# Two transformer blocks on one core: projections of the delta rule spaced with empty steps, SiLU as one ScalarE operation, and five moves of weight products

## The chip, the cores and the metric

The kernel runs on one core of a Trainium2 chip. The metric is the device time of one execution in microseconds (us), the median over runs. In the text PE is the matrix engine (TensorE), PEld its weight load, ACT the scalar engine, DVE the vector engine, POOL the GpSimd engine and SP the queue that issues transfers.

## What is computed

Two transformer blocks in series on a sequence of 512 tokens with 1024 features, all in float32. The first block has stick-breaking attention, forgetting attention and a memory attention, merged by gates, and an MLP. The change touches only the second block, which is, cut to what matters:

```
h  = rmsnorm(x)
qa, ka, va, za, alpha, beta, qb, kb, vb, ga, gb = split(h @ w_in)
qa, ka, va = silu(causal_conv4(qa, ka, va))            # 8 heads of 128, silu(x) = x * sigmoid(x)
oa = gated_deltanet(qa, ka, va, alpha, beta)           # chunks of 64: S = a S + k^T (v - k S)
oa = rmsnorm(oa) * silu(za)
ob = band_attention(qb, kb, vb, bias)                  # 16 heads of 64
x += (sigmoid(ga) * (oa @ w_a_out) + sigmoid(gb) * (ob @ w_b_out)) @ w_o
x += memory_cross_attention(rmsnorm(x), rmsnorm(mem))  # 4 heads of 256, 256 memory tokens
x += (silu(gate) * up) @ w_down
```

## The kernel before

Every weight product is one `Gemm`: a tile of 128 output features by 512 tokens, summed over eight blocks of 128 input features. Float32 accuracy comes from three passes for each block, with weights and activations split in a high and a low part: lines 1034 (high by high), 1036 (weights high, activations low) and 1040 (weights low, activations high). Weights come in units of eight blocks. SP loads a unit into `stage`, ACT makes the high part (line 1477, `whi`), and DVE or POOL subtracts to make the low part (`wlo`); in the delta rule it is POOL (line 2331). The split of the next unit stands in the queues of ACT and POOL at the first block of a product.

The order of the work is written out by hand. `Schedule` yields steps, which are lists of operations with a name; a step can be an empty list. Every engine walks the same flat list and takes its part of each operation, so the queue of every engine has the order of the list. `mix` takes one step from each of its parts in turn. `par` makes lists of its parts and spreads each evenly over their common length, so that it is the number of steps in each list, empty ones too, that decides which operation stands beside which. A product has four `mm` steps (two blocks, six matmuls each) and one `ev` step, the eviction from PSUM on DVE.

For the delta rule `block2` (line 807 on) runs nine rounds. Round h holds in one `par`: `gdn_scan(h-1)` with 24 steps, `gdn_prep(h)` with 13 and `gdn_proj(h+1)` with 45. Round 0 has no scan, round 7 has instead of a projection a few gate products, round 8 has the last scan and five gate products.

- `gdn_scan`: for each of eight chunks `gc_w` (two matmuls of the state with wt and with qd on PE, then on DVE `cuu`, line 1855) and `gc_s` (two matmuls with ckd and cuu on PE, then on DVE the new state `cs`, line 2213 or 1858). Each needs the one before, through DVE. Below W2 is `gc_w` of chunk 2, S2 its `gc_s`. Then comes a norm and the product with silu(z) on POOL.
- `gdn_prep`: `gp_kk`, `gp_xy`, five times `gp_P` and `gp_Y` (16 or 32 small matmuls on PE, then multiplications and subtractions on tiles `ya` on DVE), and `gp_uw`, 32 matmuls. Below P1 and Y1 are the first pair. With P1 go the scores of q and k, and on DVE `ceg`, `cqd` and `cpt`.
- `gdn_proj`: `products` yields the products of k, q, v and z in this order; `chain`, mixed with it, yields empty steps until a product is there, then the convolution `conv` on DVE in two steps (lines 2130 and 1858: part 0 has one `tensor_scalar` and one `scalar_tensor_tensor`, part 1 two of the latter), `silus` and the norms `hn_sq`, `hn_mm`, `hn_out` of k and q. `silus` gives a `sig` step (ACT, line 1722, into the buffers `ce`) and a `silu` step for each item (POOL, line 2331, times the sigmoid). `later(h-1)` is the one for v and z of the head before.

The scan's `gc_w` and `gc_s` share PSUM bank 7 with the norms of k and q.

Around the delta rule: `gdn_scalars` turns the alpha and beta columns, after one first product, into decays; `gdn_in` with its small matmuls opens it. `gated("a2")` with `opened` multiplies the delta output with `w_a_out`; `opened` starts two products up to their sixth block, since the last two blocks need the last head. In the band attention eight pairs of heads run each beside the three products of the next pair; pairs 3 to 7 have also one or two gate products (`raw_gate`). In `xattn` all 16 key and value products of the memory run first; then four heads of cross attention, the first two of them beside the query products of heads 2 and 3.

Of the kernel before, what the change touches and what calls it, by code (L numbers as in the profile page):

```python
# [12 lines left out]
ACT = mybir.ActivationFunctionType  # L13
# [358 lines left out]
class Schedule:  # L372
# [15 lines left out]

    def raw_gate(self, name, col, out, ph):

        return self.gemm(name, col, range(8), ("H", ph), "h", None, [("dve_ev", (name, col, 0))], extra=[Use(f"raw{col}", [])], out=out)

    def gate(self, name, col, out, place, ph):
        return self.gemm(name, col, range(8), ("H", ph), "gate", place, [("dve_ev", (name, col, 0))], out=out)
# [194 lines left out]
    def gated(self, tag, ph, gates, branches, bufs, pre, late=False):  # L589
        n, mg = 0, {"b1": "mg1", "b2": "mg2"}.get(tag)  # L590
        if tag == "a2":
            yield from self.opened(tag, branches, bufs, pre)
        for m in range(2 if tag == "a2" else 0, 8):
            A = bufs[2 + m % 2]
            uA = Use(f"{tag}acc{m % 2}", [("gt_copy", m)] if tag == "a2" else [("sp_hi", (mg, m)), ("sp_lo", (mg, m))])
            for j, ((gname, gcol), (bname, src, nk)) in enumerate(zip(gates, branches)):
                gkey, bkey = (gname, gcol + 128 * m, 0), (bname, 128 * m, 0)
                s, t_ = pre.get((m, j), (bufs[n % 2], f"{tag}s{n % 2}"))[0], bufs[4 + n % 2]
                if late and (m, j) in pre:
                    yield [st("late_gate", (gkey, s))]  # L600
                if (m, j) not in pre:
                    yield from self.gate(gname, gcol + 128 * m, s, Use(f"{tag}s{n % 2}", [("dve_ev", bkey)]), ph)
                ut = Use(f"{tag}t{n % 2}", [("gt_add", (tag, m, j))])
                yield from self.gemm(bname, 128 * m, range(nk), src, "branch", uA if j == 0 else ut, [("dve_ev", bkey)],
                                     s=s, A=A, t=t_, j=j, tag=tag, m=m, s_key=gkey)
                n += 1
            ref = ("gt_add", (tag, m, len(gates) - 1)) if len(gates) > 1 else ("dve_ev", bkey)
            yield [st("merge", (tag, m, A, ref))]

    def opened(self, tag, branches, bufs, pre):  # L610

        (bname, src, nk), made = branches[0], []
        for m in range(2):
            A, bkey = bufs[2 + m], (bname, 128 * m, 0)
            g = self.gemm(bname, 128 * m, range(nk), src, "branch", Use(f"{tag}acc{m}", [("gt_copy", m)]), [("dve_ev", bkey)],
                          s=pre[m, 0][0], A=A, t=None, j=0, tag=tag, m=m, s_key=("w_in_2", 7184 + 128 * m, 0))
            made.append((g, [st("merge", (tag, m, A, ("dve_ev", bkey)))]))
        for g, _ in made:
            yield from islice(g, nk // 2 - 1)
        for g, merge in made:  # L620
            yield from g
            yield merge
# [64 lines left out]

    def gdn_scalars(self):
        u = Use("b5", [("gs_be", 0)])
        yield [st("gs_in", u, u)]  # L690
        yield from repeat([], 5)
        u = Use("b7", [("gs_er", 0)])
        yield [st("gs_cols", u, u)]
        ub, ub2 = Use("b7", [("gs_row", 0)]), Use("b6", [("gs_row", 1)])
        rows = [Use(f"gbc{h}", self.gbc_freed(h)) for h in range(2)]
        yield [st("gs_rows", (ub, ub2), ub, ub2)]
        yield from repeat([], 8)
        yield [st("gs_store", None)] + [st("gdn_rows", (h, rows[h]), rows[h]) for h in range(2)]
# [4 lines left out]
    def gdn_proj(self, h):  # L703

        k, s = self.k, h % 2
        done = set()
        ce = [0]

        def silus(*items):
            us = []  # L710
            for e, (n, g, buf, ref) in enumerate(items):
                us.append(Use(f"ce{e}", [("silu", (n, g))]))
            yield [st("sig", (items, us), *us), st("tables", None)]
            for e, (n, g, buf, ref) in enumerate(items):
                yield [st("silu", (n, g, buf, e))]

        def later(g):
            return silus(("v", g, k.g3[g % 2]["v"], ("conv", ("v", g))), ("z", g, k.gz[g % 3], ("dve_ev", ("w_in_2", 3072 + 128 * g, 0))))
        if h == 8:
            yield [x for s_ in later(7) for x in s_]  # L720
            for _ in range(5):
                yield []
            return

        def products():
            for n in "kqv":
                j, x = "qkv".index(n), CX[n]
                yield from self.proj("w_in_2", 128 * (8 * j + h), k.cx[x][:, 3:3 + T], Use(f"cx{x}", [("conv", (n, h))]), "mix2")
                done.add(n)
            yield from self.proj("w_in_2", 3072 + 128 * h, k.gz[h % 3][:], Use(f"gz{h % 3}", [("gs_oz", h)]), "mix2")  # L730

        freed = {"q": [("pe_qk", h), ("gp_qd", h)], "k": [("pe_ktr", h)], "v": [("pe_vtr", h)]}

        def conv(n):
            while n not in done:
                yield []
            u = Use(f"g{n}{s}", freed[n])
            yield [st("conv", (n, h, 0, u), u)]
            yield [st("conv", (n, h, 1, None))]

        def unit(n, g):
            b = k.g3[s][n][:]
            return self.norm(("l2" + n, h), b, None, b, ("silu", (n, h)), k.cf("ones"), 1.0, g)

        def chain():
            yield from conv("k")
            if h:
                yield from later(h - 1)
            yield from conv("q")
            yield from silus(*((n, h, k.g3[s][n], ("conv", (n, h))) for n in "kq"))  # L750
            yield from unit("k", 1.0)
            yield from conv("v")
            yield from unit("q", 128 ** -0.5)
        yield from mix(products(), chain())
# [52 lines left out]
    def block2(self):  # L807
# [32 lines left out]

        early = {}

        def gates(*ms):
            for m in ms:
                early[m, 0] = k.bgate[m][:], None
            return [(self.raw_gate("w_in_2", 8208 + 128 * m, k.bgate[m][:], "mix2"), None) for m in ms]
        beside = [[], [], [], gates(0), gates(1), gates(2), gates(3), gates(4, 5)]

        def band_loads(p):
            for h in (2 * p, 2 * p + 1):  # L850
# [37 lines left out]
    def xattn(self):  # L888
        k = self.k
        yield [st("tables", None)]  # L890

        def proj(i):
            for j in range(2):
                s = 2 * (i % 3) + j
                yield from self.proj("w_mq_2", 256 * i + 128 * j, k.xq[s][:], Use(f"xq{s}", [("pe_xo", (i, 1)), ("pe_xo", (i, 3))]), "x2")
        yield from par(seq(proj(0), proj(1)), self.mem_norm(2, "norm_mem_2"))
        yield from self.mem_kv(2, "w_mkv_2", k.raw2, 8, k.mk2, k.mv2, None, range(16))
        self.xo = [[Use(f"b{6 + j}", [("o_hi", ("o3", 2 * i + j)), ("o_lo", ("o3", 2 * i + j))]) for j in range(2)] for i in range(4)]
        for i in range(4):
            yield from par(self.cross(i, 0), self.cross(i, 1), *([proj(i + 2)] if i < 2 else []))  # L900
            yield [st("xa_out", i)]
        yield from self.residual("w_mo_2", "o3", range(8), "ffn", "norm_ffn_2", ("w_mq_2", 896, 0))
        yield [st("fence", "ff2")]
# [551 lines left out]
def scalar_program(k, act):  # L1455
# [261 lines left out]

    def sigmoids(items, uses):
        for e, (n, g, buf, ref) in enumerate(items):
            free(uses[e])  # L1720
            wait(ref)
            act.activation(k.ce[e][:], buf[:], ACT.Sigmoid).then_inc(*up("sig", (n, g)))

    def prep_eg(h, u):
        free(u["eg"])
# [590 lines left out]
def pool_program(k, pool):  # L2316
# [64 lines left out]
        pool.wait_ge(*at("dc_sub", (h, mask)))  # L2381
        tt(k.gD, k.gD, k.cb(mask), ALU.add).then_inc(*up("dc_mask", (h, mask)))

    def silu(n, g, buf, e):
        pool.wait_ge(*at("sig", (n, g)))
        tt(buf[:], buf[:], k.ce[e][:], ALU.mult).then_inc(*up("silu", (n, g)))

    def scan_gate(h):
        wait(("silu", ("z", h)))
# [4 lines left out]
    for kind, a in k.order:  # L2394
# [7 lines left out]
        elif kind == "ev":  # L2402
            evict(a)
        elif kind == "merge":
            merge(*a)
        elif kind == "decay":
            decay(*a)
        elif kind == "silu":
            silu(*a)
        elif kind == "gs_oz":  # L2410
            scan_gate(a)
        elif kind == "band_load":
            h, _ = a
            pool.wait_ge(*at("ld_band%d" % (h % 4), h))
            pool.memset(k.band[h % 4][0:64, 0:64], NEG).then_inc(*up("band", h))
        elif kind == "fence":
            for e in ("pe", "act", "dve"):
                if k.tails.get((a, e)):
                    name, n = k.tails[a, e]
                    pool.wait_ge(k.sem(name), n)  # L2420
            k.tails[a, "pool"] = hand.tail
# [159 lines left out]
```

## Time and profile before

| what | value |
|---|---|
| median of 3 runs | 2320.1 us (2319.35 to 2322.78) |
| the profiled execution | 2320.81 us |
| its span, first to last instruction | 2319.0 us |
| granted clock of PE, mean | 0.996 |
| busy: PE, DVE, ACT, POOL | 97%, 49%, 39%, 19% |
| the chain that ended last | PE 87%, DVE 6%, ACT 3%, issue 2%, DMA 1% |
| the first block, to the fence `gdn` | to about 936 us |
| delta rule | about 936 to 1385 us |
| output product of the delta rule | about 1385 to 1430 us |
| band attention | about 1432 to 1675 us |
| products of the memory's keys and values | about 1780 to 1845 us |
| cross attention | about 1845 to 1902 us |

A row of the timeline gives the start in us from the beginning of the span, the duration in us, the engine, the line, the operation, what it writes and reads, how many instructions are merged in it, and in brackets how long the engine was idle before it and on which instruction that wait ended. A busy PE counts the tail of a matmul too, so that an idle time is given some 0.1 us too short. Which of PE's two clock levels was granted is the column PEclk: 1.00 is 2.4 GHz, 0.50 is 1.2 GHz.

### The profile page before, as it was taken

How to read it: one execution, taken by the hardware profiler on the slowest of the kernel's cores; microseconds unless marked ns; L12 is line 12 of the kernel's file. 1: busy time of each engine (PE TensorE's matmuls, PEld its weight loads, DVE VectorE, ACT ScalarE, POOL GpSimd, SP SyncE). 2: the span in 40 equal slices, each digit the busy share in tenths (PEclk: the TensorE clock that was granted, in tenths of full speed). 3: DMA queues.
4: the chain of work that ended last, by engine and by line, in shares of the span. 5: the costliest groups of instructions: out<-in, count | busy, mean ns of one | idle time of the engine just before them, and what ended most of it. 6: DMA issues, size and time to landing. Idle time of an engine off the chain costs nothing.

```text
span 2319.0 us, 32779 instructions
## 1 busy us (share of the span) xinstructions
PE 2254.3 (97%) x13098; PEld 1798.2 (78%) x13098; DVE 1141.5 (49%) x1949; ACT 892.9 (39%) x1427; POOL 443.7 (19%) x300
## 2 busy tenths in 40 slices
PE   8999999999999999999999999999999999999998
PEld 6776777888888888777777777777788988888886
DVE  4433454444544445575666512555546445435444
ACT  5544564233322223434443442444434434222223
POOL 2332221001201102444353332000011001101001
PEclk9999999999999999999999999999999999999999
DMA  4223212323333233221121123222232513233322
GB/s 166 73 64 101 64 46 82 100 92 99 93 98 101 92 99 92 95 71 47 47 70 51 38 66 128 81 82 83 63 100 92 155 37 100 91 100 100 98 93 82
DMA packets 58358, 198.95 MB, mean 86 GB/s; under 512 B 6736, under 2 KB 6864, under 8 KB 57952
## 3 DMA queue, kind: packets, MB, share of 16 engines
q1 hardware_dynamic: 58208, 196.86, 27.0%
q8 instruction: 105, 1.72, 0.3%
q14 instruction: 45, 0.37, 0.1%
HBM read 194.67 MB, written 2.16 MB: 85 GB/s over the span
## 4 chain that ended last, share of the span: by engine, by line
PE 87%; DVE 6%; ACT 3%; issue 2%; DMA 1%; POOL 0%; SPq 0%; DVEq 0%; ACTq 0%; POOLq 0%
PE bank L1034 24%; PE bank L1040 24%; PE bank L1036 24%; PE bank L989 13%; PE bank L992 2%; ACT whi L1477 1%; DMA stage<-in_wall 1%; DVE ya L1855 1%; DVE gk L1858 1%; DVE wlo L1855 0%; DVE gk L2130 0%; DVE sbA L2032 0%; SPq L2430 0%; DVE gq L1858 0%; DVE gv L1858 0%
## 5 line engine op out<-in xcount | busy, mean ns | idle before, releaser
L1034 PE MATMUL bank<-hh,whi 128*128 128x512 f32 x1680 | 688.0, 410 | 1.1 <-ACT nm1r L1517 0.6
L1040 PE MATMUL bank<-hh,wlo 128*128 128x512 f32 x1680 | 658.1, 392 | 4.8 <-DVE wlo L1855 3.1
L1036 PE MATMUL bank<-hl,whi 128*128 128x512 f32 x1680 | 656.0, 390 | 0.0
L1477 ACT ACTIVATE whi<-stage 128x1024 fp32r<-128x1024 f32 x340 | 357.3, 1051 | 326.5 <-PE bank L1040 315.5
L1855 DVE TENSOR_TENSOR wlo<-stage,whi 128x1024 fp32r<-128x1024 f32 x252 | 331.5, 1316 | 295.6 <-ACT whi L1477 295.1
L1040 PEld LDWEIGHTS bank<-hh,wlo 128*128 128x128 f32 x1680 | 315.9, 188 | 75.9 <-DVE wlo L1855 5.7
L1034 PEld LDWEIGHTS bank<-hh,whi 128*128 128x128 f32 x1680 | 316.5, 188 | 73.2 <-issue 9.3
L1036 PEld LDWEIGHTS bank<-hl,whi 128*128 128x128 f32 x1680 | 316.8, 189 | 63.6 <-issue 5.3
L2331 POOL TENSOR_TENSOR wlo<-stage,whi 128x1024 fp32r<-128x1024 f32 x88 | 210.6, 2393 | 408.1 <-ACT whi L1477 408.1
L1855 DVE TENSOR_TENSOR x<-bank,x 128x512 f32<-128x512 f32 x80 | 55.3, 691 | 152.6 <-PE bank L1040 152.6
L2331 POOL TENSOR_TENSOR acc<-acc,sqb 128x512 f32<-128x512 f32 x34 | 45.2, 1329 | 288.9 <-ACT sqb L1490 288.9
L1034 PE MATMUL bank<-u1h,whi 128*128 128x512 f32 x256 | 99.6, 389 | 0.0
L1036 PE MATMUL bank<-u1l,whi 128*128 128x512 f32 x256 | 99.6, 389 | 0.0
L1040 PE MATMUL bank<-u1h,wlo 128*128 128x512 f32 x256 | 99.6, 389 | 0.0
L2331 POOL TENSOR_TENSOR u1l<-f1t,u1h 128x512 fp32r<-128x512 f32 x32 | 41.3, 1292 | 265.2 <-ACT u1h L1575 265.2
L2331 POOL TENSOR_TENSOR u2l<-f2s,u2h 128x512 fp32r<-128x512 f32 x22 | 28.4, 1293 | 299.7 <-ACT u2h L1584 299.7
L989 PEld LDWEIGHTS bank<-ya 64*64 64x64 f32 (+1 forms) x2048 | 58.9, 138 | 32.2 <-issue 16.5
L989 PE MATMUL bank<-ya 64*64 64x64 f32 (+2 forms) x2048 | 72.4, 231 | 5.9 <-DVE ya L1855 5.8
L1575 ACT ACTIVATE u1h<-f1t 128x512 fp32r<-128x512 f32 x32 | 20.2, 632 | 126.6 <-DVE f1t L1855 126.6
L1036 PE MATMUL bank<-u2l,whi 128*128 128x512 f32 x176 | 68.6, 390 | 0.0
L1034 PE MATMUL bank<-u2h,whi 128*128 128x512 f32 x176 | 68.5, 389 | 0.0
L1040 PE MATMUL bank<-u2h,wlo 128*128 128x512 f32 x176 | 68.5, 389 | 0.0
(374 smaller groups left out, 3446.4 us busy)
## 6 DMA issues: line engine op xcount, KB each, us to landing
stage<-in_wall SPq DMA_DIRECT2D x340, 512.0 KB, 3.6
band<-in_toep SPq DMA_DIRECT2D x16, 256.0 KB, 3.9
x<-in_xT SPq DMA_DIRECT2D x8, 256.0 KB, 5.2
fb<-rowsf SPq DMA_DIRECT2D x8, 256.0 KB, 3.7
gbc<-rows SPq DMA_DIRECT2D x8, 256.0 KB, 3.3
gbc<-rowsc SPq DMA_DIRECT2D x16, 128.0 KB, 3.6
out_y<-fout SPq DMA_DIRECT2D x8, 256.0 KB, 2.3
memx<-in_memT SPq DMA_DIRECT2D x1, 1024.0 KB, 10.0
```

Source lines behind the costliest of these rows:

```text
L989: return pe.matmul(out, w, r, start=start, stop=stop, skip_group_check=True)
L992: return pe.transpose(out, in_, k.cf("ident"))
L1034: pe.matmul(o, wh, hi, start=j == 0, stop=False)
L1036: pe.matmul(o, wh, lo, start=False, stop=False)
L1040: i = pe.matmul(o, wl, hi, start=False, stop=end)
L1477: act.activation(k.whi[u % NSPLIT][:], k.stage[u % NSTAGE][:], ACT.Copy).then_inc(*up("whi", u))
L1575: act.activation(k.u1[0][:, a["t"] % 16, :], a["b"][:], ACT.Copy).then_inc(*up("sp_hi", ("u1", a["t"])))
L1855: return dve.tensor_tensor(out, a, b, op)
L1858: return dve.scalar_tensor_tensor(out=out, in0=a, scalar=s, in1=b, op0=op0, op1=op1)
L2331: return pool.tensor_tensor(out, a, b, op)
```

## The change

1. `raw_gate` uses PSUM bank 7 instead of the two banks that the products take in turn, and the six gate products beside the band attention are cut in pieces: three steps beside each of the pairs 0 to 6, nine beside pair 7.
2. `opened` starts four products instead of two, in banks 2 to 5.
3. `gdn_scalars` starts three steps later.
4. `silus` is one step: ACT applies `Silu` in place, POOL does nothing.
5. In `products` two empty steps stand after each of the products of k, q and v, for all heads but the first.
6. The value products 12 to 15 of the memory run beside cross head 0, and the query products of heads 2 and 3 beside cross heads 1 and 2.

```diff
     def raw_gate(self, name, col, out, ph):
...
+                         bank="b7", out=out)
...
-        for m in range(2 if tag == "a2" else 0, 8):
+        for m in range(4 if tag == "a2" else 0, 8):
...
     def opened(self, tag, branches, bufs, pre):
-        for m in range(2):
+        for m in range(4):
+            A, bkey = bufs[2 + m % 2], (bname, 128 * m, 0)
...
+                          bank=f"b{2 + m}", s=pre[m, 0][0], ...
...
     def gdn_scalars(self):
         u = Use("b5", [("gs_be", 0)])
+        yield from repeat([], 3)
         yield [st("gs_in", u, u)]
...
         def silus(*items):
             us = []
-            for e, (n, g, buf, ref) in enumerate(items):
-                us.append(Use(f"ce{e}", [("silu", (n, g))]))
-            yield [st("sig", (items, us), *us), st("tables", None)]
-            for e, (n, g, buf, ref) in enumerate(items):
-                yield [st("silu", (n, g, buf, e))]
+            yield [st("sig", (items, us)), st("tables", None)]
...
                 done.add(n)
+                if h:
+                    yield from repeat([], 2)
...
-        def gates(*ms):
-            for m in ms:
+        def gates():
+            for m in range(6):
                 early[m, 0] = k.bgate[m][:], None
-            return [(self.raw_gate("w_in_2", 8208 + 128 * m, k.bgate[m][:], "mix2"), None) for m in ms]
-        beside = [[], [], [], gates(0), gates(1), gates(2), gates(3), gates(4, 5)]
+                yield from self.raw_gate("w_in_2", 8208 + 128 * m, k.bgate[m][:], "mix2")
+        slow = gates()
+        beside = [[(islice(slow, 3), None)] for _ in range(7)] + [[(slow, None)]]
...
-        yield from self.mem_kv(2, "w_mkv_2", k.raw2, 8, k.mk2, k.mv2, None, range(16))
+        yield from self.mem_kv(2, "w_mkv_2", k.raw2, 8, k.mk2, k.mv2, None, range(12))
+        beside = [self.mem_kv(2, "w_mkv_2", k.raw2, 8, k.mk2, k.mv2, None, range(12, 16)), proj(2), proj(3), []]
...
-            yield from par(self.cross(i, 0), self.cross(i, 1), *([proj(i + 2)] if i < 2 else []))
+            yield from par(self.cross(i, 0), self.cross(i, 1), beside[i])
...
     def sigmoids(items, uses):
-            free(uses[e])
             wait(ref)
-            act.activation(k.ce[e][:], buf[:], ACT.Sigmoid).then_inc(*up("sig", (n, g)))
+            act.activation(buf[:], buf[:], ACT.Silu).then_inc(*up("silu", (n, g)))
...
-    def silu(n, g, buf, e):
-        pool.wait_ge(*at("sig", (n, g)))
-        tt(buf[:], buf[:], k.ce[e][:], ALU.mult).then_inc(*up("silu", (n, g)))
```

## Rows read from the trace of the kernel before

**Rows 1.** The page, busy time of each engine over the whole span.

```profile
PE 2254.3 (97%) x13098; PEld 1798.2 (78%) x13098; DVE 1141.5 (49%) x1949; ACT 892.9 (39%) x1427; POOL 443.7 (19%) x300
```

**Rows 2.** Busy time by stretch: start:end, length, PE, PEld, DVE, ACT, POOL, PEclk, DMA share, GB/s.

```profile
1060.50:1108.40 47.90, 45.49 (x489) 35.23 (x490) 30.82 (x58) 20.58 (x30) 20.55 (x14) 1.00 0.16 56
...
1845.00:1910.00 65.00, 61.72 (x351) 52.87 (x350) 31.63 (x83) 24.33 (x64) 0.00 (x0) 1.00 0.14 45
```

**Rows 3.** Timeline of PE in one round of the delta rule.

```profile
1069.51 0.49 PE L989 MATMUL bank<-cs,cwt 128*128 128x128 f32 x2 [0.21 <-DVE cs L2213]
...
1071.32 0.49 PE L989 MATMUL bank<-cuu,ckd 128*128 128x128 f32 x2
...
1071.79 0.48 PE L1034 MATMUL bank<-hh,whi 128*128 128x512 f32 x1
...
1073.98 0.49 PE L989 MATMUL bank<-cs,cwt 128*128 128x128 f32 x2
...
1077.22 0.46 PE L989 MATMUL bank<-cuu,ckd 128*128 128x128 f32 x2 [1.15 <-DVE cuu L1855]
...
1093.76 0.46 PE L989 MATMUL bank<-cuu,ckd 128*128 128x128 f32 x2 [0.29 <-DVE cuu L1855]
...
1106.22 2.13 PE L989 MATMUL bank<-ya 64*64 64x128 f32 x32 [0.70 <-DVE ya L1855]
```

**Rows 4.** Timeline of DVE in the same round.

```profile
1071.29 1.21 DVE L2165 COPY ceg<-ya 128x8 f32<-128x8 f32 x1
...
1073.36 0.33 DVE L1858 SCALAR_TENSOR_TENSOR cs<-cs,ceg,bank 128x128 f32<-128x128 f32 x1
1073.61 0.91 DVE L2130 TENSOR_SCALAR gk<-cx,vecs 128x512 f32<-128x512 f32 x1
1074.56 1.66 DVE L1858 SCALAR_TENSOR_TENSOR gk<-cx,vecs,gk 128x512 f32<-128x512 f32 x1
1076.14 0.74 DVE L1855 TENSOR_TENSOR ya<-ya,bank 128x256 f32<-128x256 f32 x2
1076.80 0.27 DVE L1855 TENSOR_TENSOR cuu<-cu,bank 64x128 f32<-64x128 f32 x1
1077.00 1.52 DVE L1858 SCALAR_TENSOR_TENSOR gk<-cx,vecs,gk 128x512 f32<-128x512 f32 x2
...
1104.57 0.48 DVE L2130 TENSOR_SCALAR gv<-cx,vecs 128x512 f32<-128x512 f32 x1
1105.09 0.75 DVE L1858 SCALAR_TENSOR_TENSOR gv<-cx,vecs,gv 128x512 f32<-128x512 f32 x1
```

**Rows 5.** Timeline of POOL in the same round.

```profile
1070.09 2.38 POOL L2331 TENSOR_TENSOR wlo<-stage,whi 128x1024 fp32r<-128x1024 f32 x1 [1.47 <-ACT whi L1477]
1072.42 1.82 POOL L2331 TENSOR_TENSOR gv<-gv,ce 128x512 f32<-128x512 f32 x1
```

**Rows 6.** Timeline of PE, idle times in rounds 0 and 7 and outside the delta rule.

```profile
40.48 0.49 PE L989 MATMUL bank<-sbA,cft 128*128 128x128 f32 x2 [1.98 <-DVE sbA L1858]
...
941.16 1.06 PE L989 MATMUL bank<-cft,ya 16*128 16x16 f32 x8 [2.22 <-DVE ya L1858]
...
1009.11 2.54 PE L989 MATMUL bank<-ya 64*64 64x128 f32 x32 [1.69 <-DVE ya L1855]
...
1314.17 0.46 PE L989 MATMUL bank<-cuu,ckd 128*128 128x128 f32 x2 [0.55 <-DVE cuu L1855]
...
1387.70 0.50 PE L1040 MATMUL bank<-oah,wlo 128*128 128x512 f32 x1 [1.79 <-POOL wlo L2331]
...
1469.92 1.09 PE L989 MATMUL bank<-bdpt,bv 128*64 128x128 f32 x16 [0.89 <-ACT bdpt L1637]
...
1885.22 1.13 PE L989 MATMUL bank<-mk,xq 128*128 128x256 f32 x4 [1.52 <-ACT xap L1663]
```

**Rows 7.** Busy time by stretch, six us from two of these idle times on, columns as in Rows 2.

```profile
941.00:947.00 6.00, 5.84 (x22) 4.85 (x23) 1.42 (x9) 2.08 (x7) 1.41 (x1) 0.72 0.28 83
1009.00:1015.00 6.00, 5.89 (x40) 4.21 (x40) 1.47 (x3) 2.47 (x5) 0.00 (x0) 0.72 0.01 3
```

More of the change, by code:

```diff
@@ L389, in raw_gate @@
     def raw_gate(self, name, col, out, ph):
-        return self.gemm(name, col, range(8), ("H", ph), "h", None, [("dve_ev", (name, col, 0))], extra=[Use(f"raw{col}", [])], out=out)
+        return self.gemm(name, col, range(8), ("H", ph), "h", None, [("dve_ev", (name, col, 0))], extra=[Use(f"raw{col}", [])],
+                         bank="b7", out=out)
     def gate(self, name, col, out, place, ph):
@@ L612, in opened @@
         (bname, src, nk), made = branches[0], []
-        for m in range(2):
-            A, bkey = bufs[2 + m], (bname, 128 * m, 0)
-            g = self.gemm(bname, 128 * m, range(nk), src, "branch", Use(f"{tag}acc{m}", [("gt_copy", m)]), [("dve_ev", bkey)],
-                          s=pre[m, 0][0], A=A, t=None, j=0, tag=tag, m=m, s_key=("w_in_2", 7184 + 128 * m, 0))
+        for m in range(4):
+            A, bkey = bufs[2 + m % 2], (bname, 128 * m, 0)
+            g = self.gemm(bname, 128 * m, range(nk), src, "branch", Use(f"{tag}acc{m % 2}", [("gt_copy", m)]), [("dve_ev", bkey)],
+                          bank=f"b{2 + m}", s=pre[m, 0][0], A=A, t=None, j=0, tag=tag, m=m, s_key=("w_in_2", 7184 + 128 * m, 0))
             made.append((g, [st("merge", (tag, m, A, ("dve_ev", bkey)))]))
@@ L2407, in pool_program @@
             decay(*a)
-        elif kind == "silu":
-            silu(*a)
         elif kind == "gs_oz":
```

## The prediction

> **What bounds the kernel now.** I read the page first: PE is busy for 2254.3 of 2319.0 us [rows 1]. No other engine is near that, and the change removes no work of PE. So it can only win or lose PE's idle time, some 65 us in all, and the time in which PE has the low clock. The next view is busy time by stretch: one round of the delta rule takes 47.9 us with PE busy for 45.5, so 2.4 us are idle; the cross attention loses 3.3 of 65 [rows 2]. The timeline of PE then shows which idle times these are. In a round there are four, always the same ones in rounds 1 to 6: 0.21 before chunk 1's `gc_w`, 1.15 before chunk 2's `gc_s` (S2), 0.29 before chunk 6's and 0.70 before `gp_uw`; 2.35 us together [rows 3]. All end on DVE. What counts is thus the order of DVE's queue and which PE work stands beside each hand-over.
>
> **POOL's products (part 4).** Four products by the sigmoid leave POOL in every round, 1.5 to 1.8 us each [rows 5]. Nobody on PE waits for them. What they do is hold DVE: while POOL multiplies v and z [rows 5], two operations of conv k take 0.91 and 1.66 us instead of 0.48 and 0.75 [rows 4], and those 1.34 us stand ahead of the `cuu` that S2 waits for. The Trainium skill, SBUF — State Buffer, section "SBUF: two separate sides", calls the pair of ports that the two engines share an exclusive lock, held for the whole instruction; by that rule alone the wait of 1.15 us goes and the six rounds win 6.9 us. The trace agrees on the lock, but the rule says nothing of what the new order puts in its place. `Silu` itself is not in the trace. On ACT it replaces a sigmoid one for one, with the same changes of table if its table costs what the other does. From below its cost is nothing; from above, if it took as long again as the removed product (1.8 us), its result would come when it comes now. I take no change.
>
> **The empty steps (part 5).** I count steps. `silus` shrinks from three to one, but `chain` waits for the products, which now have 26 steps; the list goes from 45 to 51, against 24 of the scan and 13 of the preparation. Spread by `par`, the old order begins
>
> k0, kk, k1, k2, xy, k3, S0, W1, ev k, P1, S1, **q0, conv k part 0**, Y1, W2, **q1**, conv k part 1, S2, q2 ...
>
> (q0 is the first `mm` step of q), which is what PE shows: S1 at 1071.32, a product at 1071.79, W2 at 1073.98, S2 late at 1077.22 [rows 3]. The new one is
>
> k0, kk, k1, k2, xy, k3, S0, ev k, W1, P1, **conv k part 0**, S1, **conv k part 1**, Y1, W2, **q0**, S2, q1 ...
>
> Two things change. Conv k part 0 is now ahead of the state update of S1 in DVE's queue, and no product fills PE between S1 and W2. Walk it with durations of this round. POOL's split still holds `ceg` for 1.21 us to the same moment [rows 4, 5]. The state update started at 1073.36; now 0.48 + 0.75 come first, so it starts near 1074.6 and ends near 1074.9, and W2 can start near 1075.0. PE is through S1 (0.47, to 1071.79 [rows 3]) and Y1 (some 0.6, from what lies between 1071.79 and 1073.98 beside a product step of 1.5) at 1072.4. From there to 1075.0 are 2.6 us, some **2.4 us** as the rows count idle time, where there was none. S2 then needs conv k part 1 (1.52), two subtractions (0.74) and `cuu` (0.27) [rows 4]: ready near 1077.4, PE there at 76.9 after W2 and q0, 0.4 idle.
>
> The rest of the new round, from the same count: W4 directly before S4, behind Y2 (the same sequence costs 0.55 in round 7 [rows 6]); S5 behind conv q; P5 directly behind Y4; and `hn_mm k` directly behind W7, whose bank 7 it needs. For these three the trace has no row; the nearest is the bare hand-over of 0.29 [rows 3], and the bounds are 0 and 0.7 each. I take 0.3. On the good side z's steps now reach the end of the round: the 0.70 before `gp_uw` and the 0.29 before S6 go. Sum after: 0.21 + 2.4 + 0.4 + 0.55 + 0.9 = 4.45 us, against 2.35: **+2.1 for a round, +12.6 for six**. Bounds for the term of 2.4: 0.3, if DVE has slack that I don't see, and 3.0.
>
> Round 0 has no scan, and waits 1.69 before `gp_uw` [rows 6], with a low clock behind it. That wait is filled, but both parts of conv k now come between P1 and Y1's subtractions (2.7 us of DVE, one product step less beside them: some 2 us before P2), and P5, Y5 wait some 1.3: +1.6, with the clock alike (bounds 0 and +3). Round 7 keeps its order and loses POOL's lock: -0.6.
>
> **The clock.** An idle PE has a second price. After 2.22 and 1.69 us of idleness [rows 6] the granted clock over the next six us was 0.72 [rows 7], a mix of 2.4 and 1.2 GHz, which is 0.28 x 6 = 1.7 us lost. After 1.79 and after 1.52 us [rows 6] it stayed at 2.4 GHz. The new wait of 2.4 us is longer than all of these. Where the clock falls, the 0.4 us before S2 are swallowed: +1.3. I take four rounds of six, +5.2; bounds 0 and +10. The Trainium skill, TensorE: Matmul & The Clock Gate, "Part 1", says that the gate follows how busy PE was lately, in a rhythm of its own that does not start with the kernel. By that rule the same stall would fall on both sides, as 1.69 and 1.79 do here.
>
> **Start (part 3).** `gdn_in` stalled PE for 2.22 us and the clock fell for 1.7 [rows 6, 7]. Two product steps now stand before it and cover this. They need their low part from POOL earlier than before, and `gs_rows` loses the product that stood before it. Between nothing won and 3.9, I take -2.2.
>
> **The other moves.** `opened` (part 2): PE's wait there, 1.79 us [rows 6], is for the split of the second unit behind ACT's queue. That unit is due after the same eight blocks with two products or four. Nothing changes: 0 (bounds -1 and 0). Band (part 1): the wait of 0.89 before the last values product [rows 6] occurs in pairs 0 to 2, which have no gate product. With three steps each, by the count of 21 steps against 16, pairs 1 and 6 have an eviction at that place and not matmuls, so two such waits are left: -0.9 (bounds -2.7 and +0.5, for a turn that takes the next product's bank). Cross attention (part 6): heads 2 and 3 wait 1.52 each [rows 6]; head 2 gets cover, head 3 not, and the memory's last turn gets cover too: -2.0 (bounds -1 and -3). The weights' low parts come from DVE there and keep pace, as DVE is busy for 31.6 of 65 us [rows 2].
>
> **Sum:** 12.6 + 1.6 - 0.6 + 5.2 - 2.2 + 0 - 0.9 - 2.0 = +13.7 us. It is made against the profiled execution, 2320.8 us (span 2319.0 and 1.8 around it), which is 0.7 above the median of 2320.1. So the forecast is 2333.8 us in terms of that median.
>
> **Rivals.** A measurement of this kernel can tell some 0.2% from no change, 4.6 us.
>
> (a) The walk is right, but the clock holds at 2.4 GHz in rounds 1 to 6: 2320.1 + 8.5 = 2328.6. For it speaks the row of 1.79 us; against it, that the wait is longer than each one that brought the clock down.
>
> (b) Faster: the lock was what held PE. Freed of POOL's products, DVE has done conv k before PE comes to W2, the wait is 0.3 us instead of 2.4, and the covered ends of the rounds are the gain. Then a round is at +0.0, without the three small waits at -0.9; six give -3 (mean of both), the clock does not fall, and with round 0 even, start, band, cross and round 7 give -5.7: 2311. It decides in favour of faster when the wait before W2 is below some 1.0 us (4.1 us won elsewhere, divided by six, is 0.7 for a round, which is 1.4 below my +2.1). For it: the 0.91 and 1.66 [rows 4]. Against: I have used the short durations, and it is the place in the queue that costs.
>
> (c) Slower still: the wait before W2 is 3.0 and the clock falls in all six rounds: 8.5 + 3.6 + 7.8 = +20: 2340.
>
> (d) The terms cancel: waits trade places in the queue, a round at +1, no clock loss: 2320.1 + 1.9 = 2322. This is also where it lies if the spacing does not act as counted.
>
> **Chances:** forecast 0.42, (a) 0.20, (b) 0.15, (c) 0.13, (d) 0.10. The forecast's own range is 2329 to 2338. To leave out no more than 2 in 10 the range goes from 2317.5, which takes in (d) and cuts off (b), to 2344. Faster 0.15; same 0.12, (d) and the lower edge of (a); slower 0.73.
>
> **What would show it.** Right: PE idle some 2.4 us before the matmuls of `cs` and `cwt` of chunk 2 in each of rounds 1 to 6, ended by DVE's `cs`; conv k's two first operations ahead of that `cs` on DVE, at 0.48 and 0.75 us; no wait before `gp_uw`; rounds of 50 to 51 us instead of 47.9; a granted clock below 1.00 in several rounds; no idle 2.22 us at the start; one wait of 1.52 left in the cross attention. The prediction is wrong if rounds are shorter than 47.9 us, if the wait before W2 is below 1 us, or if `gp_uw` still waits.

## The result, and the profile after

The changed kernel takes 2353.4 us (median of 4 runs, 2351.3 to 2355.1), the kernel before 2320.9 in runs beside it: a ratio of 1.0137 [1.0125, 1.0149], +32.5 us. The forecast was 2333.8, the range ended at 2344.0. The direction was right, the size less than half of what came. The profiled execution took 2352.8 us, its span is 2351.0, against 2319.0.

The page, busy time of each engine over the whole span, kernel after; it answers to [rows 1].

```profile
PE 2266.2 (96%) x13098; PEld 1805.8 (77%) x13098; DVE 1135.7 (48%) x1949; ACT 895.4 (38%) x1427; POOL 401.9 (17%) x268
```

PE has the same 13098 instructions and is busy for 11.9 us more, in the main by the lower clock (mean 0.991 against 0.996). The other 20.1 us of the longer span are idle time of PE. POOL has lost 32 instructions and 41.8 us, which nobody on PE waited for.

I cut both traces into stages, at the first or last instruction of PE that touches a certain tile. Each cell is the length in us and, in brackets, PE's idle time in it:

```
stage (predicted difference)          before         after          difference
up to the delta rule's scalars        932.2          933.1            +0.9
start of the delta rule (-2.2)         42.4 (3.6)     39.6 (2.7)      -2.8
round 0 (+1.6)                         40.7 (1.7)     41.9 (4.9)      +1.3
rounds 1 to 6 (+12.6 and +5.2)        286.9 (14.2)   309.5 (26.8)    +22.6
rounds 7 and 8 (-0.6)                  76.0 (3.8)     75.1 (2.8)      -0.9
product of the delta output (0)        46.2 (2.7)     48.9 (2.7)      +2.7
band attention (-0.9)                 225.2 (2.9)    234.5 (8.8)      +9.3
memory and cross attention (-2.0)     108.1 (4.5)    106.9 (3.7)      -1.2
all else                              561.3          561.5            +0.1
```

**A round of the delta rule.** First PE's timeline, the waits of the round that begins at 1065.20 and its S1; these answer to [rows 3].

```profile
1071.85 0.49 PE L991 MATMUL bank<-cs,cwt 128*128 128x128 f32 x2 [0.21 <-DVE cs L2214]
...
1073.67 0.49 PE L991 MATMUL bank<-cuu,ckd 128*128 128x128 f32 x2
...
1077.09 0.79 PE L991 MATMUL bank<-cs,cwt 128*128 128x128 f32 x2 [2.14 <-DVE cs L1859]
...
1090.91 0.46 PE L991 MATMUL bank<-cuu,ckd 128*128 128x128 f32 x2 [0.55 <-DVE cuu L1856]
...
1095.19 0.46 PE L991 MATMUL bank<-cuu,ckd 128*128 128x128 f32 x2 [0.60 <-DVE cuu L1856]
...
1103.14 1.10 PE L991 MATMUL bank<-sqb,cft 128*128 128x512 f32 x2 [0.30 <-DVE cuu L1856]
...
1105.55 0.68 PE L991 MATMUL bank<-ya 64*64 64x64 f32 x16 [0.53 <-DVE ya L1856]
```

The waits of 1.15 and 0.70 of [rows 3] are gone, W2 waits 2.14, and its two matmuls take 0.79 instead of 0.49: the clock has fallen. DVE's timeline at that place, which answers to [rows 4]:

```profile
1073.24 0.42 DVE L1856 TENSOR_TENSOR ya<-bank,cft 128x256 f32<-128x256 f32 x1 [0.52 <-PE bank L991]
1073.58 1.09 DVE L2166 COPY ceg<-ya 128x8 f32<-128x8 f32 x1
1074.59 0.68 DVE L1856 TENSOR_TENSOR cqd<-gq,ya 128x512 f32<-128x512 f32 x1
1075.19 0.41 DVE L1856 TENSOR_TENSOR cpt<-bank,ya 128x256 f32<-128x256 f32 x1
1075.52 0.47 DVE L2131 TENSOR_SCALAR gk<-cx,vecs 128x512 f32<-128x512 f32 x1
1076.03 0.75 DVE L1859 SCALAR_TENSOR_TENSOR gk<-cx,vecs,gk 128x512 f32<-128x512 f32 x1
1076.70 0.34 DVE L1859 SCALAR_TENSOR_TENSOR cs<-cs,ceg,bank 128x128 f32<-128x128 f32 x1
```

The two operations of conv k have their short durations, since POOL's product is no longer beside them, but both now stand ahead of the state `cs`. ACT's timeline in the same round shows the new operation; before, the table took 1.28 and the sigmoid 0.63 at this place as well.

```profile
1072.23 1.28 ACT L1723 ACT_TABLE_LOAD   x1
1073.52 0.63 ACT L1723 ACTIVATE gv<-gv 128x512 f32<-128x512 f32 x1
1074.06 0.61 ACT L1723 ACTIVATE gz<-gz 128x512 f32<-128x512 f32 x1
1074.69 1.28 ACT L1473 ACT_TABLE_LOAD   x1
```

**The stages.** Busy time by stretch, kernel after, columns as in [rows 2]: rounds 0 to 6, the product of the delta output, the band attention, rounds 1, 2 and 3, a part of the band attention.

```profile
972.70:1324.60 351.90, 320.20 (x3371) 247.46 (x3372) 207.75 (x393) 144.05 (x201) 104.26 (x68) 0.97 0.17 54
1399.70:1448.60 48.90, 46.18 (x191) 37.32 (x190) 10.17 (x16) 11.53 (x13) 21.93 (x10) 0.93 0.25 76
1469.90:1704.40 234.50, 225.67 (x1279) 163.69 (x1278) 133.46 (x388) 101.99 (x240) 1.75 (x12) 0.99 0.25 75
1014.64:1065.20 50.56, 45.77 (x489) 35.27 (x488) 29.90 (x58) 20.31 (x30) 14.29 (x10) 1.00 0.18 53
1065.20:1118.06 52.86, 48.47 (x490) 37.79 (x489) 29.99 (x58) 20.84 (x30) 15.33 (x11) 0.94 0.17 51
1118.06:1169.65 51.59, 47.19 (x489) 36.37 (x488) 29.85 (x58) 20.82 (x30) 15.32 (x11) 0.97 0.16 52
1550.00:1580.00 30.00, 27.48 (x144) 20.26 (x143) 15.13 (x44) 11.58 (x26) 0.29 (x2) 0.94 0.27 88
```

Rounds 3 to 6 take 51.5 to 51.6 us with a mean clock of 0.97, against 47.9 at 1.00 before: in each the clock is at 1.2 GHz for a stretch. In round 2 this stretch is longer (0.94, 52.9 us). In round 1 there is none: PE waits 2.15 us before W2 there as well, but the clock stays at 1.00 and the round takes 50.6 us.

**The band attention.** PE's groups of instructions there (from 1460 to 1700 us), kernel after, those that wait: out<-in, shapes, count, busy us, mean ns, idle us before and what ended it.

```profile
L1036 PE MATMUL bank<-hh,whi 128*128 128x512 f32 x222 | 92.0, 414 | 3.8 <-ACT bv L1558 3.4 <-ACT whi L1479 0.3
...
L994 PE MATMUL bank<-cft,bdp 128*128 128x128 f32 x152 | 24.1, 286 | 3.6 <-DVE bdp L2033 3.6
L991 PE MATMUL bank<-bdpt,bv 128*64 128x128 f32 x292 | 23.3, 290 | 1.8 <-ACT bdpt L1639 1.8
```

Before, the first matmul of a product never waited here, the transposes of `bdp` waited 0.2 in all, and the values products 2.7 for `bdpt`. The new 3.4 are five waits of 0.69, each before the first matmul of a q product, for ACT's copy of the values:

```profile
1564.38 0.50 PE L1036 MATMUL bank<-hh,whi 128*128 128x512 f32 x1 [0.69 <-ACT bv L1558]
...
1595.08 0.50 PE L1036 MATMUL bank<-hh,whi 128*128 128x512 f32 x1 [0.69 <-ACT bv L1558]
```

### The profile page after: what moved, and what is told of

Its sections match the earlier page's. It is cut to its first block, busy times and chain, and to the rows that moved or that the text cites. A ratio compares the mean times of both kernels' runs of the same rounds, so it can differ in the third digit from the quotient of the medians.

```text
span 2351.0 us, 32717 instructions
## 1 busy us (share of the span) xinstructions
PE 2266.2 (96%) x13098; PEld 1805.8 (77%) x13098; DVE 1135.7 (48%) x1949; ACT 895.4 (38%) x1427; POOL 401.9 (17%) x268
## 3 DMA queue, kind: packets, MB, share of 16 engines
q1 hardware_dynamic: 58208, 196.86, 26.8%
## 4 chain that ended last, share of the span: by engine, by line
PE 52%; DVE 4%; issue 2%; ACT 2%; POOL 0%; DMA 0%; DVEq 0%; SPq 0%; ACTq 0%; POOLq 0%
PE bank L1036 14%; PE bank L1042 14%; PE bank L1038 13%; PE bank L991 9%; PE bank L994 2%; DVE ya L1856 1%; ACT whi L1479 1%; DVE wlo L1856 0%; DVE gq L1859 0%; DMA stage<-in_wall 0%; DVE cuu L1856 0%; DVE cqd L1856 0%; POOL wlo L2332 0%; DVE fout L1856 0%; DVE gk L1859 0%
```

## The experiments

The first four undo or isolate parts, with 3 rounds of runs against the kernel before on one chip; that kernel had a median of 2321.1 us there. The other four had one chip with 2320.4.

**1. Without the spacing (part 5).** The changed kernel without these lines:

```diff
-                if h:
-                    yield from repeat([], 2)
```

> The changed kernel without the empty steps behind the products of k, q and v; all else as changed (the list has 43 steps). Theory A (the empty steps set the loss: a product leaves the place between S1 and W2, and conv k comes ahead of the state update): a product stands there again, the wait before W2 falls from 2.14 us to under 0.5, the clock stays at 2.4 GHz, rounds 1 to 6 fall from 51.6 to about 47.5 us, and the time from 2353 to about 2330 us. Rival B (the one-step Silu, or the other moves, set it): rounds stay above 50 us, the time stays above 2345.

Measured: 2324.5 us, 1.0012 [1.0002, 1.0022], 5.5 less than I expected; rounds of 47.7 us with 2.2 idle and the clock at 1.00. So the spacing costs 28.9 us of the 32.5. One expectation failed: W2 still waits 1.06, where I had under 0.5. With `silus` shortened and no empty steps the list has 43 steps, and again the order shifts: the eviction of k comes behind P1's work on DVE. DVE's timeline of that kernel, at the same place:

```profile
1067.82 2.04 DVE L2164 COPY ceg<-ya 128x8 f32<-128x8 f32 x1
...
1070.71 0.68 DVE L1857 SCALAR_TENSOR_TENSOR cx<-bank,rr 128x512 f32<-128x512 f32 x1
1071.30 0.33 DVE L1857 SCALAR_TENSOR_TENSOR cs<-cs,ceg,bank 128x128 f32<-128x128 f32 x1
```

The small copy `ceg` is held for 2.04 us here: POOL's split runs from 1067.44 to 1069.82 in this kernel, and the copy ends with it, at 1069.86. The same holds in the changed kernel, with 1074.65 and 1074.67. The Trainium skill, SBUF — State Buffer, section "SBUF: two separate sides", has the one engine fully blocked for the other's whole instruction; the trace agrees for this copy.

**2. With the old band attention (part 1 undone).** `raw_gate` without `bank="b7"`, and the old `gates` and `beside`.

```diff
-                         bank="b7", out=out)
-        beside = [[(islice(slow, 3), None)] for _ in range(7)] + [[(slow, None)]]
+        beside = [[], [], [], gates(0), gates(1), gates(2), gates(3), gates(4, 5)]
```

> The changed kernel with the gate products of the band attention put back as before (whole, beside pairs 3 to 7, in the alternating banks). Theory A (the slices cost the 9.4 us that the band attention takes longer): the band attention is back at 241 us, the time at about 2344 us. Rival B (the band attention is slower because of what comes ahead of it, a shifted clock or later loads): it stays at 250 us and the time at 2353.

Measured: 2342.4 us, 1.0092 [1.0077, 1.0107], 11.0 less than with the change; the band attention is back at 225.2 us with 2.9 idle (the 241 and 250 of the expectation are for a wider cut of the same stage). The product of the delta output, whose code this kernel has unchanged, took 46.1 us instead of 48.9, with the same idle time of 2.7: these 2.8 are the clock.

**3. The spacing alone.** The kernel before with the empty steps of part 5 and nothing else; POOL's products stay.

```diff
                 done.add(n)
+                if h:
+                    yield from repeat([], 2)
```

> The kernel before with the empty steps alone; the sigmoid on ACT and the product on POOL stay, and so do their steps. Theory A (the empty steps are the cause whatever POOL does): rounds of 51 to 53 us, a granted clock below 1.00 in them, time 2341 to 2350 us. Rival B (only together with the shortened silus list do they move the order to the bad place): rounds below 49 us, time below 2328.

Measured: 2380.9 us, 1.0254 [1.0239, 1.0269]. Here I was far too low. Rounds are 55.2 to 58.1 us with 8.3 idle. PE's wait before W2 is 3.87 us; DVE's timeline shows why, and POOL's below it:

```profile
1085.11 1.15 DVE L2132 TENSOR_SCALAR gk<-cx,vecs 128x512 f32<-128x512 f32 x1
1086.30 1.63 DVE L1860 SCALAR_TENSOR_TENSOR gk<-cx,vecs,gk 128x512 f32<-128x512 f32 x1
1087.85 0.33 DVE L1860 SCALAR_TENSOR_TENSOR cs<-cs,ceg,bank 128x128 f32<-128x128 f32 x1
```

```profile
1084.19 1.79 POOL L2333 TENSOR_TENSOR gv<-gv,ce 128x512 f32<-128x512 f32 x1
1085.94 1.44 POOL L2333 TENSOR_TENSOR gz<-gz,ce 128x512 f32<-128x512 f32 x1
```

Conv k stands ahead of the state and is held by POOL's products as well. The order and the lock are not two prices that add: the lock makes what stands ahead longer. A second wait of 2.31 us, before S5, lies behind it; the changed kernel has 0.61 there.

**4. `Silu` alone, with the old order.** The kernel before with `Silu` on ACT, and POOL's steps kept as empty ones.

```diff
-            yield [st("sig", (items, us), *us), st("tables", None)]
-            for e, (n, g, buf, ref) in enumerate(items):
-                yield [st("silu", (n, g, buf, e))]
+            yield [st("sig", (items, us)), st("tables", None)]
+            yield from repeat([], len(items))
```

> The kernel before with Silu as one operation of ACT, the two steps of POOL's products kept as empty steps, so that the order of all else is unchanged. Theory A (POOL's products hold DVE by a lock and DVE's lateness holds PE): conv k takes 0.48 and 0.75 us instead of 0.91 and 1.66, the wait of 1.15 us before S2 is gone, rounds take about 46.7 us instead of 47.9, time about 2313 us. Rival B (the lock costs nothing on the path): rounds stay at 47.9, time 2320 to 2322.

Measured: 2311.4 us, 0.9955 [0.9941, 0.9970]. A round takes 46.5 us with 1.26 idle: the 1.15 before S2 is gone and nothing has taken its place. One steady round and the seven rounds 0 to 6 of this kernel, busy time by stretch:

```profile
973.50:1291.90 318.40, 309.18 (x3372) 239.34 (x3372) 198.12 (x394) 141.55 (x200) 99.46 (x67) 1.00 0.18 59
1105.40:1151.90 46.50, 45.24 (x490) 35.17 (x490) 28.47 (x58) 20.56 (x30) 14.63 (x10) 1.00 0.17 58
```

This is the gain that the change holds and hides. Rounds 1 to 6 take 279.1 us instead of 286.9, with 7.5 idle instead of 14.2: -7.8, where the 1.15 us alone were priced at 6.9. Round 0 is 1.8 shorter with the same wait of 1.68 in it, and the start 2.6, with the wait of 2.22 before `gdn_in` as in [rows 6]; at neither did the clock fall here. The product of the delta output took 48.9, 2.7 more.

**5. Another bank for the values' turn.** The changed kernel; the gate products, which have bank 7, don't count in the turn of the two product banks.

```diff
-            if kind == "mm" and what[1] == 0:
+            raw = kind in ("mm", "ev") and (what if kind == "ev" else what[0]).use.place == "b7"
+            if kind == "mm" and what[1] == 0 and not raw:
                 gi += 1
-            if kind in ("mm", "ev"):
+            if kind in ("mm", "ev") and not raw:
                 ended = kind == "ev"
```

> The changed kernel, but the raw gate products, which have bank 7, no longer count in the turn of the two product banks, so that the turn of the values takes the bank that the next pair's q product does not. Theory (the 9.3 us that the band attention lost are in part this bank: five first products of q wait 0.69 us for ACT's copy bv, and each wait helps the clock down): these five waits are gone, the stage falls from 234.5 to some 230.5 us, the kernel to about 2349. The rest of the loss, the four waits for bdp and bdpt before the values products and some of the clock, stays, since it comes from the number of steps. Rival 1 (the bank is innocent, ACT is late for the copy in any bank and the next matmuls wait in its place): the stage stays at 234 to 235, the kernel at 2353. Rival 2 (the clock alone: with 3.4 us of waits gone it holds throughout): the stage at 228 or less, 2346. Rounds of the delta rule as in the changed kernel, 51.5 us.

Measured: 2346.8 us, 1.0113 [1.0098, 1.0129]. PE's groups in the band attention, the same three, and the stretch:

```profile
L1037 PE MATMUL bank<-hh,whi 128*128 128x512 f32 x226 | 93.3, 413 | 0.5 <-ACT whi L1480 0.5
...
L995 PE MATMUL bank<-cft,bdp 128*128 128x128 f32 x160 | 25.2, 285 | 3.6 <-DVE bdp L2034 3.6
L992 PE MATMUL bank<-bdpt,bv 128*64 128x128 f32 x320 | 24.5, 282 | 1.8 <-ACT bdpt L1640 1.8
```

```profile
1471.00:1699.20 228.20, 222.81 (x1279) 162.48 (x1278) 133.30 (x388) 101.75 (x240) 1.73 (x12) 1.00 0.25 77
```

The waits for `bv` are gone, those for `bdp` and `bdpt` are the same to a tenth, and the clock held throughout. Of the 9.3 us, 6.3 were the bank. Laid side by side, instruction by instruction, the two traces come apart by 0.93 us at each of the five waits, 4.6 us together, and by 1.6 us in one stretch of low clock just behind 1558 us, which only the changed kernel has here. So a row's idle time of 0.69 stands for 0.93 us of delay: it is 0.24 too short here, more than the some 0.1 that I gave above. The result is nearest to the second rival; I had let part of the clock's loss stay.

**6. Work in the place of the wait.** The changed kernel; eight matmuls of constants into the bank of the coming q product ahead of the wait before W2, in rounds 1 to 6 (`fill` is that bank).

```diff
+        if n == 2 and h < 6:
+            free(u["fill"])
+            for _ in range(8):
+                mm(bank[u["fill"].bank][:, 0:128], k.cf("ones"), k.cf("ident"), True, True)
         wait(("gc_s", (h, n - 1)))
```

> The changed kernel with eight matmuls of constants (128 columns, float32, some 0.24 us each, 2 us together) on PE ahead of the wait for the state before W2, in rounds 1 to 6; nothing reads them. They start when PE comes to the wait and end at about the moment when DVE's state is there. Theory (the idle 2.1 us bring the clock down, which costs 1.6 us a round beside the wait itself): the clock is 1.00 in the rounds, a round takes 49.8 to 50.2 us instead of 51.5, the kernel about 2344 (2342 to 2346), though PE does more. Rival (the clock falls for what the whole round gives PE, or the longer round comes from something else, such as DVE's or ACT's queue): the rounds stay at 51.5 or get longer, the kernel at 2353 to 2356.

Measured: 2344.4 us, 1.0102 [1.0089, 1.0116]. The timeline of PE and one steady round:

```profile
1074.40 2.05 PE L995 MATMUL bank<-cft 128*128 128x128 f32 x16
1076.62 0.49 PE L995 MATMUL bank<-cs,cwt 128*128 128x128 f32 x2 [0.16 <-DVE cs L1867]
```

```profile
1115.20:1165.70 50.50, 47.80 (x507) 37.16 (x506) 29.82 (x58) 20.84 (x30) 15.35 (x11) 1.00 0.18 53
```

W2 starts no earlier against S1 (3.43 us behind it, 3.42 in the changed kernel), and PE does 2.05 us more work. Still the round is 1.0 us shorter, because the clock stays at 2.4 GHz; rounds 1 to 6 take 302.8 us instead of 309.5. Round 1, where the clock had not fallen, is the check: it takes 50.5 us with the filler and 50.6 without. The round is not at 50.0 as expected: the 0.29 before S2, which the low clock had covered, is back. The rest of the 9.1 us is not the filler's: 2.1 less lie ahead of the delta rule and 1.2 less in the product of the delta output, and round 0 took 1.6 more.

**7. Conv k one place later.** The changed kernel with one more empty step before conv k, the list still at 51 steps.

```diff
         def chain():
+            while "k" not in done:
+                yield []
+            if h:
+                yield []
             yield from conv("k")
```

> The changed kernel with one more empty step in the chain before conv k, in rounds 1 to 6; conv k's two parts come one place later (behind S1 and behind q0), all else stays where it is, and the list has 51 steps as before. Theory (W2 waits because conv k part 0, 1.23 us, stands ahead of the state update on DVE): the wait before W2 falls from 2.14 to some 0.9 us, the clock stays at 1.00, a round takes some 48.8 us, the kernel 2335 to 2339. Rival (W2's wait comes from the missing product between S1 and W2, and DVE is busy with ceg, cqd and cpt at any rate): the wait stays at 1.9 to 2.1 us, the rounds at 51.5, the kernel at 2352 to 2354. A third (the wait moves to S2, which now has conv k part 1 right ahead of its subtraction): the wait before W2 0.9 but that before S2 1.2 or more, a round 49.8 to 51.

Measured: 2332.4 us, 1.0050 [1.0036, 1.0064], 21.0 less than the changed kernel; 15.3 of them are rounds 1 to 6 (294.2 instead of 309.5), for one place in DVE's queue. DVE and PE at the place, and one steady round:

```profile
1071.72 0.41 DVE L1860 TENSOR_TENSOR cpt<-bank,ya 128x256 f32<-128x256 f32 x1
1072.05 0.33 DVE L1863 SCALAR_TENSOR_TENSOR cs<-cs,ceg,bank 128x128 f32<-128x128 f32 x1
1072.31 0.47 DVE L2135 TENSOR_SCALAR gk<-cx,vecs 128x512 f32<-128x512 f32 x1
```

```profile
1072.44 0.49 PE L995 MATMUL bank<-cs,cwt 128*128 128x128 f32 x2 [0.96 <-DVE cs L1863]
```

```profile
1110.70:1159.70 49.00, 45.75 (x489) 35.27 (x488) 29.76 (x58) 20.78 (x30) 15.31 (x11) 1.00 0.17 55
```

The wait fell by 1.18 us, which is conv k part 0 (0.47 and 0.75, overlapping a little). The clock held, and S2 did not wait. The kernel came out 2.6 us below the range that I had given; round 0 gained too, where the wait before P2 fell from 2.68 to 1.09.

**8. The best of the parts.** The kernel of experiment 4 with part 3 (the scalars three steps later) and part 6 (the memory's and the cross attention's products); no spacing, the old band attention, two opened products.

> The kernel before with Silu on ACT (the removed POOL steps kept as empty ones, no other empty steps), the scalars of the delta rule three steps later, and the four value products of the memory and the query products of heads 2 and 3 moved beside the cross attention; not the band's gate pieces, not four opened products, not the spacing. Theory: the sum of what its parts gave: Silu alone 2311.4, the cross attention 1.2 less, the start nothing more (it was 39.8 us with Silu alone and 39.6 in the changed kernel): 2310 (2308.5 to 2311.5), ratio 0.995. Rival (the moves beside the cross attention and at the start bring waits of their own when the split's pace is another): 2312 or more.

Measured: 2307.7 us, 0.9947 [0.9935, 0.9960] over 5 rounds, 12.7 us below the kernel before and 0.8 below the range that I had given. The start took 38.8 us, 1.0 less than in experiment 4, the cross attention 106.9 against 108.1.

## Why the prediction was right in direction and wrong in size

**The empty steps: right, step by step.** The idle time of rounds 1 to 6 rose by 26.8 - 14.2 = 12.6 us, and the forecast was 12.6. That they agree to the tenth is luck, since in five rounds the low clock covers the wait before S2; with the clock held it would be 14.0. The order was read off the count of steps, and conv k ahead of `cs` was there in each round. Term by term: W1 0.21 (0.21), W2 2.14 (2.4), S2 0 (0.4), S4 0.55 (0.55), S5 0.61 (0.3), `hn_mm k` 0.31 (0.3), P5 0.53 (0.3). Two small terms were low and two high. The wait before S2 is 0.28 in round 1, where the clock is high, and covered in the rest, as the text said it would be where the clock falls. `gp_uw` no longer waits.

**The lock: right.** Experiment 4 shows the 1.15 us gone with POOL's products, experiment 3 shows them back and worse. Rival (b) had the mechanism but not the price of the new order: the decision point was a wait below 1.0 us before W2, and it was 2.14. That point was itself wrong: in experiment 7 the wait is 0.96, and the kernel is still 12.0 us slower than the kernel before, with rounds of 49.0 us and the band attention at 234.3.

**The clock in the rounds: the term was mis-sized.** I took four rounds of six at 1.3 us each, +5.2. The clock fell in five, and cost 6.7. That is read against experiment 6, where W2 starts at the same place of the round and the clock holds: 309.5 - 302.8, which is 2.4 in round 2 and 1.0 to 1.1 in each of rounds 3 to 6. This is net of the wait before S2, which the low clock covers. The other 15.9 of the 22.6 us are the order with the clock held, for which I had 12.6: 14.0 of idle time as the rows count it, and 1.9 that they leave out, because the end of the matmul before each added wait counts as busy. Experiments 6 and 7 show that it is the wait of 2.14 that brings the clock down: filled with work, or shortened to 0.96, it leaves the clock at 1.00, with the waits before S4, S5, `hn_mm k` and P5 unchanged. It does not do so each time, as round 1 shows.

**Band attention: the step that failed.** It stood at -0.9, bounds -2.7 and +0.5, and came to +9.3. I had named the mechanism in brackets, a turn that takes the next product's bank, and priced it as one wait. The bank follows a counter which each gate product moved, and with a gate product in pieces beside every pair the turn falls on the wrong bank in five pairs. Experiment 5 shows it: 6.3 us. The part that I had counted came as counted: the values products wait 1.8 instead of 2.7, 0.89 in each of pairs 1 and 6. What I had not seen, besides the bank, is that the transposes of `bdp` wait 3.6 instead of 0.2, which with the -0.9 makes the 3.0 that stay. These waits are 1.83, 0.64 and 0.89 in pairs 2, 3 and 4 and 0.25 in the last; before, pairs 3 and 4 had a whole gate product and no wait there. By the count, 21 steps stand against 16 instead of 23, one step fewer between DVE's `bdp` and its transposes. That is read from the order and not tried, and pairs 0, 1, 5 and 6 have the same 21 steps without such a wait, so the cause of these 3.4 us stays open. I looked in [rows 6] for a wait that the change would fill, and did not walk the new order of a pair as I had walked a round.

**The product of the delta output: +2.7 that the change need not have made.** The waits are the same 0.93 and 1.79. With four opened products this stage took 46.1, 47.5, 47.7 (three times) and 48.9 us in six kernels with the same code there; with two it took 46.2 in two kernels, 48.8 and 48.9 in two others. The idle time was 2.7 in all ten. So opening four does nothing that can be seen, as predicted, and the clock falls or does not fall at the same wait. The Trainium skill, TensorE: Matmul & The Clock Gate, "Part 1", says that the gate keeps a rhythm which does not start with the kernel; the runs agree, in these two to three microseconds. I had used that rule in words and left it out of the range: a stage with unchanged code can differ by 2.7 us from one trace to the next. Whether it is the shift in time by the change, or merely another execution, is not shown, since each kernel has one trace. The second could be enough by itself: up to the delta rule's scalars, where all ten kernels have the same code, the traces take 930.8 to 933.8 us, and the runs of the kernel before go from 2319.0 to 2323.6.

**Start, round 0, cross attention: about right in size, in part by luck.** The start -2.8 (-2.2), round 0 +1.3 (+1.6), rounds 7 and 8 -0.9 (-0.6), cross attention -1.2 (-2.0). For the start, experiment 4 has a start of 39.8 us with the wait of 2.22 still in it, at a clock of 1.00. So 2.6 of the 2.8 can come without part 3. With it, and the clock at 1.00 as well, the start took 39.6 in the changed kernel, where `hn_mm k` waits 1.62 later on, and 38.8 in experiment 8: part 3 itself is worth 0.2 to 1.0 us. Here a right number had a wrong reason.

Round 0 is luck as well. I had +1.6 with the clock alike. The idle time rose by 3.2, twice that: P2 waits 2.68 (I had 2), four waits of 0.17 to 1.02 come with it, and the old 1.69 is gone. But the fall of the clock behind the old wait of 1.69 [rows 7] did not come, and gave about 1.7 back. In experiments 5 and 6 the clock did fall in this round, and it took 43.5 us, 2.9 more than before. In the cross attention one of the two waits of 1.52 is gone, as forecast; the wait of 0.53 for the memory's turn stays, and one of 0.81 before the transposes of `xap` is new.

**The sum.** The span grew by 32.0 us where 13.7 were forecast. Of the 18.3 that were missing, 10.2 are the band attention (9.3 against -0.9), 4.8 rounds 1 to 6 (22.6 against 17.8: 3.3 the order, 1.5 the clock), 2.7 the product of the delta output; the rest is 0.6.

## What to carry to other kernels

Where a list is spread by its number of steps, removing work also removes places. Keep the places (experiment 4, -7.8 us in six rounds) or walk the new order in full, in every stage whose count changes; one place in DVE's queue was worth 15.3 us, 8.6 of them without the clock (294.2 against the 302.8 of experiment 6) and 6.7 with it. Price an idle time of about two microseconds on PE as two prices, the wait and the clock, and a bank or buffer chosen by a counter as a part of the change as soon as anything that counts is moved.

## What the runs showed that I had not expected

Idle matrix time can be worth filling with work that nobody needs: 2.05 us of it in each of six rounds made them 6.7 us shorter together (experiment 6).

The length of a wait alone does not say whether the clock falls. That of 2.22 us before `gdn_in` brought it to 0.72 over six us in the kernel before [rows 7], and left it at 1.00 in experiment 4. That of 2.14 or 2.15 before W2 brought it down in five rounds of six in the changed kernel and in six of six in experiments 2 and 5. That of 2.68 in round 0 left it at 1.00 in the changed kernel, and in experiments 5 and 6 it fell.

A lock on DVE is not a fixed price. The copy `ceg` of 128x8 elements took 1.09, 1.21 and 2.04 us, by where POOL's split of 2.38 us began; the first operation of conv k took 0.47, 0.91 and 1.15.
